# Hybrid recurrent decoder: split weights kept in HBM for the second token block, and a POOL subtraction in two halves

## The reference, cut to what matters

```python
for layer in range(DEPTH):                      # 2 layers
    hn = rmsnorm(x, norm_mix[layer])
    mix, ... = mixer_even(hn, ...) if layer % 2 == 0 else mixer_odd(hn, ...)
    x = x + mix                                 # mixer: (hn @ w_in), recurrences, @ w_out
    x = x + swiglu(rmsnorm(x, norm_ffn[layer]), ffn_w_up[layer], ffn_w_down[layer])
...
def swiglu(h, w_up, w_down):
    g, u = jnp.split(h @ w_up, 2, axis=-1)
    return (jax.nn.silu(g) * u) @ w_down        # d_ff = 2816
```

## Time and profile before

| what | value |
|---|---|
| median of 3 runs | 2495.21 us (2494.74 to 2500.96) |
| the profiled execution | 2493.78 us |
| its span in the profile | 2492.0 us, mean granted clock 0.992 |
| TensorE busy | 2432.9 us |
| POOL busy | 1252.7 us |
| DMA traffic | 235.18 MB |

### The profile page before, as it was taken

One profiled execution on the slowest core, in us unless ns is written; L12 is line 12 of the kernel. 1 busy time (PEld: TensorE's weight loads), 2 busy tenths in 40 slices (PEclk: granted clock), 3 DMA queues, 4 the chain that ended last, 5 costly groups with the idle time before them and its releaser, 6 DMA issues.

```text
span 2492.0 us, 36702 instructions
## 1 busy us (share of the span) xinstructions
PE 2432.9 (98%) x15510; PEld 2193.5 (88%) x15510; DVE 1007.6 (40%) x1712; ACT 934.2 (37%) x1219; POOL 1252.7 (50%) x669
## 2 busy tenths in 40 slices
PE   8999999899999999999999999999999999999998
PEld 6889987688887877999999889988887889999998
DVE  4513245334445434543333443454434454222224
ACT  5342345233223455443333254544432335222223
POOL 3745455555455644544354473344445556544453
PEclk9999999999999999999999999999999999999999
DMA  5322233321323222222222222222233323222222
GB/s 184 102 82 69 71 130 97 115 77 60 123 85 119 92 90 92 88 74 94 85 77 94 77 88 87 85 95 75 86 101 107 126 86 127 92 88 93 94 85 86
DMA packets 74594, 235.18 MB, mean 94 GB/s; under 512 B 9216, under 2 KB 13120, under 8 KB 74432
## 3 DMA queue, kind: packets, MB, share of 16 engines
q1 hardware_dynamic: 74432, 232.84, 27.9%
HBM read 221.64 MB, written 9.05 MB: 93 GB/s over the span
## 4 chain that ended last, share of the span: by engine, by line
PE 86%; DVE 5%; POOL 2%; issue 2%; ACT 2%; POOLq 1%; DVEq 1%; DMA 1%; SPq 0%; ACTq 0%
PE ps L761 62%; PE ps L816 17%; POOL wl L1380 1%; DMA wr<-in_wblk 1%; PE ps L912 1%; PE ps L910 1%; PE ps L856 1%; ACT wh L1114 1%; PE ps L785 0%; DVE sq L1550 0%; DVE mixl L1764 0%; POOL sq L1486 0%; PE ps L973 0%; POOLq L1397 0%; PE ps L970 0%
## 5 line engine op out<-in xcount | busy, mean ns | idle before, releaser
L1380 POOL TENSOR_TENSOR wl<-wr,wh 128x1024 fp32r<-128x1024 f32 x392 | 943.3, 2420 | 592.2 <-ACT wh L1114 591.7
L761 PE MATMUL ps<-xh,wh 128*128 128x260 f32 (+2 forms) x3296 | 882.5, 322 | 8.1 <-DVE qk L1552 4.2
L761 PE MATMUL ps<-xl,wh 128*128 128x260 f32 (+2 forms) x3296 | 869.0, 318 | 0.0
L761 PE MATMUL ps<-xh,wl 128*128 128x260 f32 (+1 forms) x3280 | 867.1, 319 | 0.0
L761 PEld LDWEIGHTS ps<-xh,wh 128*128 128x128 f32 (+1 forms) x3296 | 544.4, 188 | 61.6 <-issue 18.8
L761 PEld LDWEIGHTS ps<-xl,wh 128*128 128x128 f32 (+1 forms) x3296 | 543.7, 188 | 44.9 <-issue 2.4
L761 PEld LDWEIGHTS ps<-xh,wl 128*128 128x128 f32 x3280 | 541.9, 188 | 44.6
L1114 ACT ACTIVATE wh<-wr 128x1024 fp32r<-128x1024 f32 (+2 forms) x396 | 410.0, 1045 | 393.8 <-DMA wr<-in_wblk 389.2
L816 PE MATMUL ps<-hidh,wh 128*128 128x260 f32 (+1 forms) x1024 | 279.9, 327 | 21.8 <-POOL wl L1380 9.5
L1239 ACT ACTIVATE sq<-sq 128x512 f32<-128x512 f32 (+1 forms) x88 | 55.9, 636 | 609.0 <-DVE sq L1550 609.0
L816 PE MATMUL ps<-hidl,wh 128*128 128x260 f32 (+1 forms) x1024 | 276.3, 323 | 0.0
(11 more groups left out here) (373 smaller groups left out, 2316.9 us busy)
## 6 DMA issues: line engine op xcount, KB each, us to landing
wr<-in_wblk SPq DMA_DIRECT2D x392, 512.0 KB, 3.4
xr<-in_xT SPq DMA_DIRECT2D x8, 260.0 KB, 5.8
xB<-in_xT SPq DMA_DIRECT2D x8, 260.0 KB, 5.8
out_yT<-xB SPq DMA_DIRECT2D x8, 260.0 KB, 2.2
xr<-in_xT SPq DMA_DIRECT2D x8, 256.0 KB, 6.0
xA<-in_xT SPq DMA_DIRECT2D x8, 256.0 KB, 4.4
Ss<-in_s_even SPq DMA_DIRECT2D x1, 2048.0 KB, 10.1
out_ss_even<-Ss SPq DMA_DIRECT2D x1, 2048.0 KB, 9.2
```

The lines of the kernel that those rows point to most:

```text
L761: mm = pe.matmul(ps[0:cols, b + c, 0:n], wt[:, w], xt[:, e:e + n], start=first, stop=end)
L1380: pool.tensor_tensor(lo, raw, hi.bitcast(F32), ALU.subtract).then_inc(s_lo, 1)
```

## The change

Blocks that are used a first time (the 196 of the A passes) are loaded and split as before, but POOL's subtraction of a block is two instructions of 512 columns instead of one of 1024, with the semaphore on the second. Two items after block n-2's own load, right behind `("w", n)`, stands a new item `("ws", n-2)`: SP waits until both parts of block n-2 are made, and stores `wh` and `wl` to a new HBM tensor `split`, 512 KB each. Blocks that are used a second time (the 196 of the B passes) are not loaded raw and not split: SP loads `wh` and `wl` from `split`, two loads of 512 KB, TensorE waits for these loads directly, and ACT and POOL do nothing for them. A load into a slot waits besides until the stores out of that slot have landed (`s_ws`).

```diff
+            if x[0] == "w" and x[1] > 2 and x[1] - 2 in kept:
+                items.append(("ws", x[1] - 2))
...
             def weights(n):
                 if n >= 4:
                     sp.wait_ge(s_unit, pl.end[n - 4] + 1)
+                    ge(sp, s_ws[n % 4], pl.stores[n - 4])
                 s = pl.blocks[n]
+                if pl.second[n]:
+                    sp.dma_start(wh[n % 4][:].bitcast(F32), a["split"][s, 0]).then_inc(s_w[n % 4], 16)
+                    sp.dma_start(wl[n % 4][:].bitcast(F32), a["split"][s, 1]).then_inc(s_w[n % 4], 16)
+                    return
...
+            def store(n):
+                sp.wait_ge(s_hi, pl.splits[n])
+                if n < 3:
+                    sp.wait_ge(s_lod, n + 1)
+                else:
+                    sp.wait_ge(s_lo, pl.splits[n] - 3)
+                s = pl.blocks[n]
+                sp.dma_start(a["split"][s, 0], wh[n % 4][:].bitcast(F32)).then_inc(s_ws[n % 4], 16)
+                sp.dma_start(a["split"][s, 1], wl[n % 4][:].bitcast(F32)).then_inc(s_ws[n % 4], 16)
...
             def weights_ready(u):
                 for n in pl.blk[u]:
-                    pe.wait_ge(s_hi, n + 1)
+                    if pl.second[n]:
+                        pe.wait_ge(s_w[n % 4], pl.loads[n])
+                        continue
+                    pe.wait_ge(s_hi, pl.splits[n])
...
             def weights_hi(n):
+                if pl.second[n]:
+                    return
...
             def weights_lo(n):
-                if n < 3:
+                if n < 3 or pl.second[n]:
                     return
...
-                pool.tensor_tensor(lo, raw, hi.bitcast(F32), ALU.subtract).then_inc(s_lo, 1)
+                for e in (slice(0, w // 2), slice(w // 2, w)):
+                    last = pool.tensor_tensor(lo[:, e], raw[:, e], hi[:, e].bitcast(F32), ALU.subtract)
+                last.then_inc(s_lo, 1)
```

More of the change, by code:

```diff
@@ L355, in __init__ @@
                 out.extend(after.get(self.u[x], ()))
-        self.items = out
+        seen, self.second = set(), {}
+        for n, s in enumerate(self.blocks):
+            self.second[n] = s in seen and not isinstance(s, tuple)
+            seen.add(s)
+        self.again = [n for n in self.second if self.second[n]]
+        self.kept = [n for n, s in enumerate(self.blocks) if not self.second[n] and not isinstance(s, tuple)]
+        self.loads, self.splits, self.stores, at, split = {}, {}, {}, [0] * 4, 0
+        stored = [0] * 4
+        for n, s in enumerate(self.blocks):
+            at[n % 4] += 32 if self.second[n] else 16
+            self.loads[n] = at[n % 4]
+            split += not self.second[n]
+            self.splits[n] = split
+            if n in self.kept:
+                stored[n % 4] += 32
+            self.stores[n] = stored[n % 4]
+        kept, items = set(self.kept), []
+        for x in out:
+            items.append(x)
+            if x[0] == "w" and x[1] > 2 and x[1] - 2 in kept:
+                items.append(("ws", x[1] - 2))
+        self.items = items
+        out = items
         assert sum(1 for x in out if x[0] == "w") == len(self.blocks)
@@ L495, in build @@
         s_w = [sem(f"w{s}") for s in range(4)]
+        s_ws = [sem(f"ws{s}") for s in range(4)]
         x_in = [sem(f"x_in{m}") for m in range(KT)]
@@ L705, in _ @@
                     weights(v[0])
+                elif k == "ws":
+                    store(v[0])
                 elif k == "dma":
@@ L713, in _ @@
                     final_half(v[0])
+            for s in range(4):
+                sp.wait_ge(s_ws[s], pl.stores[len(pl.blocks) - 4 + (s - len(pl.blocks)) % 4])
             sp.wait_ge(s_st0, 16)
@@ L734, in weights_ready @@
                     else:
-                        pe.wait_ge(s_lo, n - 2)
+                        pe.wait_ge(s_lo, pl.splits[n] - 3)
             def x_tile_ready(n, k):
@@ L1108, in weights_hi @@
             def weights_hi(n):
+                if pl.second[n]:
+                    return
                 w = block_cols(n)
-                act.wait_ge(s_w[n % 4], 16 * (n // 4 + 1))
+                act.wait_ge(s_w[n % 4], pl.loads[n])
                 raw, hi = wr[n % 4][:, 0:w], wh[n % 4][:, 0:w]
@@ L1372, in weights_lo @@
             def weights_lo(n):
-                if n < 3:
+                if n < 3 or pl.second[n]:
                     return
                 w = block_cols(n)
-                pool.wait_ge(s_hi, n + 1)
+                pool.wait_ge(s_hi, pl.splits[n])
                 raw, hi, lo = wr[n % 4][:, 0:w], wh[n % 4][:, 0:w], wl[n % 4][:, 0:w]
@@ L1379, in weights_lo @@
                     raw, hi, lo = side_by_side(n % 4)
-                pool.tensor_tensor(lo, raw, hi.bitcast(F32), ALU.subtract).then_inc(s_lo, 1)
+                    pool.tensor_tensor(lo, raw, hi.bitcast(F32), ALU.subtract).then_inc(s_lo, 1)
+                    return
+                for e in (slice(0, w // 2), slice(w // 2, w)):
+                    last = pool.tensor_tensor(lo[:, e], raw[:, e], hi[:, e].bitcast(F32), ALU.subtract)
+                last.then_inc(s_lo, 1)
             def x_squares(n, m):
@@ L2274 @@
     o = {k: nc.dram_tensor(f"out_{k}", shape, F32, kind="ExternalOutput").ap() for k, shape in _OUTS.items()}
+    a["split"] = nc.dram_tensor("split", (arrays["in_wblk"].shape[0], 2, P, D), F32).ap()
     build(nc, a, o)
```

## The result

| kernel | median, us | lowest to highest | runs | ratio to before | 95% interval |
|---|---|---|---|---|---|
| before | 2495.27 | 2492.34 to 2500.96 | 19 | 1 | |
| with the change | 2502.79 | 2496.59 to 2508.08 | 19 | 1.0029 | 1.0021 to 1.0036 |

The forecast was 2482 (2470 to 2502), 0.5% faster. The change is 0.3% slower, 0.8 us outside the range: a sum 20 us too low.

What follows compares the result with a forecast made beforehand. TensorE, busy 2432.9 of 2492.0 us, was taken as the bound, leaving only its 59 us idle and its slowed clock to win. Terms -18.8 + 2.2 + 3.8 = -12.8 us gave 2482 us (2470 to 2502).

Steps and rivals of the forecast that it cites:

- the lock: DVE operations reading two SBUF tiles stand still while POOL subtracts, so TensorE stops; B passes could give under 25 us.
- The three large stalls: TensorE's losses at 1366 to 1384, 1543 to 1556 and 820 to 832 us: 6.3, 4.8 and 3.5 us won.
- item 4: At 1426 to 1440 us, first-use subtractions stay but in halves, so DVE waits less: 0.8 us won (0 to 2).
- Item 5: FFN on A, 1988 to 2002 us: four half subtractions let DVE in sooner, 1.2 us won (0 to 1.9).
- Item 6: At 154.32 us, a POOL subtraction for the first B pass, ahead of products TensorE awaits, goes: 1.2 us won.
- Halves on A, +2.2: On A passes, two-instruction subtractions make just-in-time blocks late: 1.7 us, plus 0.5 after products of the recurrence.
- Stores in steady FFN groups on A, 0 (0 to 12): In FFN groups on A, the second `down` block's load behind stores still lands in time: cost 0, at worst 12 us.
- rival A: Stores cost what the locks give back, or B stalls only move: no change, 2488 to 2502 us, chance 0.22.
- rival B: DMA engines become the bound in dense stretches on A: slower, +56 us, 2538 us, chance 0.10.
- Large transfers that meet stores, +3.8: Stores delay loads near layer 1's sample states (+2.0 us), layer 0's states (+1.3) and the kernel's start (+0.5).

Runs made afterwards that it cites:

- reuse with the halves: The change with only four blocks stored, all B-pass loads reading those four (wrong weights), subtractions on A in halves: 2478.35 us, 0.9928 of before.
- the third store: The change without 26 blocks at the start and state transfers, plus the high part stored again to a second tensor on A: 2498.63 us, ratio 1.0017.
- the queue's order alone: The change with both 2 MB sample-state loads and the layer 0 state store issued from ACT's DMA queue, not SP's: 2493.14 us, ratio 0.9991.

## Why the prediction was wrong, point by point

- **What bounds the kernel, and the lock.** Right. The three large stalls were traced to DVE instructions held by POOL's subtractions, and they went as named, 14.6 us against 14.6. The reuse with the halves gave 17.3 against 18.8 - 2.2 = 16.6, and the ten blocks at those stalls 12.7. The Trainium skill's rule ("SBUF — State Buffer", "Who interferes with whom") held in that the stretched DVE instructions went back to their own length. Its other half, that shorter POOL instructions bound the wait, holds for single instructions (`qk` 2.82 to 1.74, the pair of `mixl` 5.50 to 3.28 with the halves alone), but is worth too little to be told in the time: halves against whole were 2494.60 against 2495.65, 2502.79 against 2503.16 and 2482.14 against 2484.35, each in favour and each within the intervals.
- **Smaller stretches.** In the last two rows of the windows of after, item 4's loss is 2.9 of idle and 1.7 of clock, 4.6 instead of 3.7: nothing was won (0.8 expected, 0 to 2). Item 5's is 0.6 instead of 1.9 (1.2 expected). Item 6, 1.2 us at the first B pass: the stop there fell from 3.8 to 2.3 us, but the clock fell too (0.99 to 0.98), and the pass kept its 183.3.
- **Halves on A, +2.2.** Too high as a sum. With the halves alone TensorE waits 3.1 us more for subtractions, the longest wait rising from 4.7 to 5.0, but DVE is free sooner, and no median shows a cost. The prediction named this second side and gave it no price.
- **Stores in steady FFN groups on A, 0 (0 to 12).** Right. In the group of the earlier trace rows the kernel after issues the load of the second `down` block at 1949.09, 11.7 us after the group's first load, as the sum had it. ACT copies the block at 1959.52, behind a silu and without a wait for the DMA, and TensorE goes past. The group before is tighter: there ACT copies the block just as it lands, 6.5 us after its issue (1910.67 to 1917.14), and TensorE doesn't stop. The upper end of the range, 12 us, doesn't follow from its own terms: 6.9 + 0.3 = 7.2, not 8.2, is 0.1 late and not 1.1. So rival A did not happen there, nor did rival B: the projections of layer 1 and both `w_out` passes on A kept their length to 0.1 us, and kept it with the third store; those of layer 0 grew by 2.3, with a stop of 2.0 at 40 us, at the start of the kernel.
- **Large transfers that meet stores, +3.8.** This is the step that failed. Measured it is 2502.8 - 2478.4 = 24 us. By the passes against the kernel that only reuses: 8.4 in the FFN with the load of `Cs` (8.5 in the run that leaves out only that place) for +2.0, 11.7 in the FFN with the states of layer 0 (454.8 against 443.1) for +1.3, and 4.6 at the start (3.0 in the first pass on A, 1.6 in the first on B) for +0.5. The prediction knew the place ("the next second `down` block arrive so late") and priced it as one pair of stores ahead, 2.7 us, and its wait. What the runs showed in its place: the block is copied 6.5 us late, 4.5 because SP issues its load late and 2.0 because it shares the engines with three pairs of stores. SP is late because it is held 3.5 us at a store that is POOL's late work, and because its issues take longer; it comes to the state's load 14.8 us after the group's first load instead of 7.5. A late block has a late store, and before 1884.19 SP waited 8.7 us for a store to land before it could fill that slot again. And each stop brings a stretch at 0.74 to 0.83 of the clock, which the prediction counted for the stalls that go, not for those that come.
- **Rival B's mechanism, in the wrong place.** "The DMA engines become the bound" was given 0.10 and ruled out by the room in steady stretches. It happened, but for 10 to 25 us at a time, where a share of 0.69 before was 0.88 after (1855 to 1877), and 0.62 was 1.02 (672 to 685). The rate in the sum, 391 GB/s, was right for blocks (376 to 419), and too high beside the output of `Cn` (299 and 153 in 1865 to 1875); no run takes that output away, so its part in the price is open. Missing was the sum of all bytes that have to pass between the state's load and the copy that is waited for. The 358 GB/s that the prediction took from the Trainium skill ("SBUF — State Buffer", "A bandwidth-pool intuition that's wrong") is under the 413 to 419 that windows of 5 us show here; over 100 us the kernel with a third store moved 357.

24 us of price and 17 us of gain make the change look like little: -17 + 24 = +7, and a choice of blocks keeps the first and sheds most of the second. Not settled: how the layer 0 price divides between the order on SP and bytes (the queue's order alone gave back 5.2 of its 11.7 us), what makes the 4.6 us at the start, and why a DMA instruction's issue on SP takes 1.2 to 2.5 us when much is in flight and 0.33 otherwise.

## What to carry to other kernels

Work taken from an engine that is not the bound was worth the locks it freed, and these stood at a few places: ten blocks of 196 brought most of the gain. Added DMA traffic cost nothing in the steady groups (1.57 MB for a block), and much beside a large transfer. There, first ask what holds the engine that issues the loads, then count all the bytes that are in flight from the transfer's issue to the next block that somebody waits for, divide by the rate, add the clock that the new stop costs, and leave these places out of the change if it doesn't come out. (No run here tried this count as a forecast.) Measure parts apart, since gain and price here were each over twice the net.

## What the runs showed of the hardware

- A DMA instruction on SP took 0.32 to 0.33 us when the queue was calm, and 1.2 to 2.5 us (2.50 at 1866.45) when several were under way.
- 16 DMA engines at a share of 0.86 moved only 153 GB/s in 1870 to 1875, while the output of `Cn` (256 KB in rows of 128 float32) was among what they carried; in two windows with next to nothing but blocks it is 413 and 419 at 1.04 and 1.03. That the rows of `Cn` are the cause is not shown.
- A DVE operation that reads two SBUF tiles ended sooner when the POOL subtraction beside it was cut in two: `qk` took 1.74 us instead of 2.82.
- Matmuls kept their rate beside DMA traffic: 100.00 of 100 us busy at 269 and at 357 GB/s, each with 427 matmuls.
